# Gating unit of a fused two-block kernel: the bias of the token mixing added by VectorE from a broadcast, in place of one-partition products on TensorE

## What is computed

```
h = gelu(x @ w_in + b_in);  u, v = split(h)
v = layernorm(v) * ln_w + ln_b
vb = v.reshape(4 blocks, 128 tokens j, 8 groups g, 128 columns c)
ws_m = ws with ws[g, i, j] = 0 where chunk(j) > chunk(i)   # chunks of 64 tokens
s[n, i, g, c] = sum_j ws_m[g, i, j] * vb[n, j, g, c] + bs[g, i]
return (u * s) @ w_out
```

## Time and profile of the kernel before

| | |
|---|---|
| Median of 3 runs | 3359.97 us (3358.32 to 3361.44) |
| The profiled execution | 3353.19 us, of which the span is 3351.4 us |
| PE busy (share of the span) | 3183.2 us (95%) |
| DVE busy | 2043.6 us (61%) |
| ACT busy | 1271.1 us (38%) |
| POOL busy | 797.8 us (24%) |
| Granted TensorE clock, mean | 0.968 |

### The profile page before, as it was taken

One profiled execution on the slowest core, in us unless ns is written; L12 is line 12 of the kernel. 1 busy time (PEld: TensorE's weight loads), 2 busy tenths in 40 slices (PEclk: granted clock), 3 DMA queues, 4 the chain that ended last, 5 costly groups with the idle time before them and its releaser, 6 DMA issues.

```text
span 3351.4 us, 42738 instructions
## 1 busy us (share of the span) xinstructions
PE 3183.2 (95%) x16817; PEld 2725.9 (81%) x16817; DVE 2043.6 (61%) x3710; ACT 1271.1 (38%) x2159; POOL 797.8 (24%) x495
## 2 busy tenths in 40 slices
PE   7878999989999999999999999999999997999999
PEld 6456989878888877888878577999999996888777
DVE  5386566564332444333257644888888774887878
ACT  4364444433232333322234433335445452333332
POOL 0000010100000020000000300477676752345553
PEclk9888999999999998999999699999999998999999
DMA  3132221133332321333322012378878888999997
GB/s 119 33 83 65 63 65 58 58 114 88 99 96 95 113 82 57 101 95 96 99 87 81 1 38 89 112 251 296 302 267 314 282 293 297 360 348 356 339 350 276
DMA packets 229210, 537.67 MB, mean 160 GB/s; under 512 B 22337, under 2 KB 88129, under 8 KB 227474
## 3 DMA queue, kind: packets, MB, share of 16 engines
q1 hardware_dynamic: 191570, 398.57, 36.0%
q0 software_dynamic: 37440, 136.36, 11.1%
HBM read 482.40 MB, written 52.46 MB: 160 GB/s over the span
## 4 chain that ended last, share of the span: by engine, by line
PE 70%; DVE 13%; DMA 8%; POOL 3%; ACT 3%; issue 2%; SPq 1%; DVEq 0%; ACTq 0%
PE bank L344 22%; PE bank L347 14%; PE bank L2200 10%; PE bank L2628 5%; DMA gl<-acts 4%; DMA eu<-in_peer_u 3%; POOL etl L2188 3%; PE bank L975 2%; PE bank L2357 2%; DVE vsl L2672 2%; PE bank L985 2%; DVE y_row L2245 2%; PE bank L939 1%; PE bank L1775 1%; PE bank L927 1%
## 5 line engine op out<-in xcount | busy, mean ns | idle before, releaser
L294 DVE TENSOR_TENSOR wl<-raw,wh 128x1024 fp32r<-128x1024 f32 (+3 forms) x239 | 294.1, 1233 | 655.3 <-ACT wh L279 655.2
L279 ACT CAST wh<-raw 128x1024 fp32r<-128x1024 f32 (+3 forms) x239 | 247.3, 1037 | 656.2 <-PE bank L344 359.0
L2188 POOL TENSOR_TENSOR etl<-eu,eth 128x1024 fp32r<-128x1024 f32 x128 | 318.8, 2492 | 435.0 <-ACT eth L2184 434.0
L2200 PE MATMUL bank<-peerhh,eth 128*128 128x384 f32 x1024 | 350.2, 342 | 30.1 <-POOL etl L2188 27.6
L2200 PE MATMUL bank<-peerhh,etl 128*128 128x384 f32 x1024 | 344.0, 336 | 0.0
L2200 PE MATMUL bank<-peerhl,eth 128*128 128x384 f32 x1024 | 344.0, 336 | 0.0
L2628 PE MATMUL bank<-vsh,coefh 128*128 128x512 f32 x768 | 302.1, 393 | 13.9 <-DVE coefl L2683 13.9
L2225 POOL DMA_INDIRECT taken<-in_peer_v,gb x128 | 250.2, 1955 | 262.0 <-DVE y_row L2245 234.7
L2628 PE MATMUL bank<-vsl,coefh 128*128 128x512 f32 x768 | 301.1, 392 | 0.0
L2628 PE MATMUL bank<-vsh,coefl 128*128 128x512 f32 x768 | 301.1, 392 | 0.0
L2184 ACT CAST eth<-eu 128x1024 fp32r<-128x1024 f32 x128 | 135.5, 1060 | 237.0 <-DMA eu<-in_peer_u 237.0
(11 more groups left out here) (544 smaller groups left out, 7457.3 us busy)
## 6 DMA issues: line engine op xcount, KB each, us to landing
eu<-in_peer_u SPq DMA_DIRECT2D x128, 512.0 KB
vb<-in_peer_v SPq DMA_DIRECT2D x128, 512.0 KB
raw<-in_ada_w SPq DMA_DIRECT2D x48, 512.0 KB, 3.8
acts<-eg SPq DMA_DIRECT2D x128, 192.0 KB
coefs<-stage SPq DMA_DIRECT2D x12, 2048.0 KB, 9.6
gd<-coefs SPq DMA_DIRECT2D x16, 1536.0 KB, 14.0
gl<-acts SPq DMA_DIRECT2D x128, 192.0 KB
raw<-in_ffn_w_gate SPq DMA_DIRECT2D x44, 512.0 KB, 3.6
```

The costliest lines, as they stand in the source:

```text
L279: act.copy(parts_of(c)[0], raw_of(c)).then_inc(*up("w rounded", c))
L294: dve.tensor_tensor(lo, raw_of(c), hi.bitcast(F32), ALU.subtract).then_inc(*up("w split", c))
L2188: pool.tensor_tensor(Et[j % 3][1], Eu[j % 2], Et[j % 3][0].bitcast(F32), ALU.subtract).then_inc(*up("u split", j))
L2200: t = pe.matmul(b, tb[un][:, k * 128:(k + 1) * 128], peer_h[hn][:, k, 1:4, :], start=k == 0 and i == 0, stop=k == 7 and i == 2)
```

## The change

The bias row `bsr` on one partition becomes `bsb`, the same 1024 values on all 128 partitions, written by one transfer of 512 KB in place of 4 KB. The 32 one-partition products are gone, and the row of ones with them. DVE gets one step more for each group: it adds the bank and the bias (repeated over the four blocks) into `btmp`, and multiplies from `btmp` in place of the bank. `btmp` has two buffers, and they are those that held v with its input bias. TensorE's bank is free after the addition, where it was free after the multiplication.

```diff
-    bsr, row1 = f("bsr", 120, 1024)[0:1, :], f("row1", 128, 128)[0:1, :]
+    bsb = f("bsb", 120, 1024)
...
-        sp.dma_start(bsr, I["sgu_bs"][0].rearrange("(o g) i -> o (g i)", o=1)).then_inc(*up("sgu in", by=16))
+        sp.dma_start(bsb, I["sgu_bs"][0].rearrange("g i -> (g i)").partition_broadcast(128)).then_inc(
+            *up("sgu in", by=16))
...
-            b, before = banks.take(("sgu s", g), ("sgu gated", g))
+            b, before = banks.take(("sgu s", g), ("dve step", "sgu mixed", g))
...
                 oc = b[:, tt * 128:(tt + 1) * 128]
-                pe.matmul(oc, row1, bsr[:, g * 128:(g + 1) * 128], start=True, stop=False, skip_group_check=True)
-                t = pe.matmul(oc, sgu_v[:, tt, g * 128:(g + 1) * 128], wsT[:, g * 128:(g + 1) * 128], start=False,
-                              stop=True, skip_group_check=True)
+                t = pe.matmul(oc, sgu_v[:, tt, g * 128:(g + 1) * 128], wsT[:, g * 128:(g + 1) * 128], start=True,
+                              stop=True)
...
-                if half == 0:
-                    dve.memset(row1, 1.0)
...
             on_dve.wait_ge(*at("bank full", "sgu mixed", g))
+            if g >= 2:
+                on_dve.wait_ge(*at("sgu gated", g - 2))
+            dve.tensor_tensor(btmp[g % 2].rearrange("p (t i) -> p t i", t=4),
+                              banks["sgu s", g].rearrange("p (t i) -> p t i", t=4),
+                              bsb[:, g * 128:(g + 1) * 128].unsqueeze(1).to_broadcast([128, 4, 128]),
+                              ALU.add).then_inc(*up("dve step", "sgu mixed", g))
+            on_dve.wait_ge(*at("dve step", "sgu mixed", g))
             on_dve.wait_ge(*at("sgu u", g))
-            dve.tensor_tensor(sgu_u[:, g, :], sgu_u[:, g, :], banks["sgu s", g],
+            dve.tensor_tensor(sgu_u[:, g, :], sgu_u[:, g, :], btmp[g % 2],
                               ALU.mult).then_inc(*up("sgu gated", g))
```

## The result

The changed kernel takes 3321.25 us (median of 4 runs, 3318.13 to 3323.63), beside 3360.7 us for the kernel before (4 runs, 3358.32 to 3363.02). The ratio is 0.9882, with a 95% interval of 0.9865 to 0.9899. In a second set of runs, on another occasion, it was 3327.02 us (6 runs) and 0.9895 (0.9874 to 0.9916). The profiled execution took 3321.01 us against 3353.19, so 32.2 us less, while the medians of the first set are 39.5 us apart and those of the second 32.0 (3359.06 before).

A forecast was written before the change was run, and what follows sets the result against it. TensorE alone was taken to bound the mixing stage. Earlier output products 34.6, their faster start 1.7, less a 0.3 wait, gave 36.0 us off the 3359.97 median: 3324.0 us, range 3320 to 3328, or 3318 to 3332 with two rivals.

The forecast's parts named there:

- The bound: Mixing stage: TensorE alone bounds its 42.3 us; the change was forecast to gain 36.0 us in all.
- The pace of what is left: Mixing stage on TensorE: the 32 remaining products take 0.24 us each, 7.7 us in all.
- The rival of 0.41 us without the bias: Mixing products keep 0.41 us each without the bias; stage 13.3 us, time 3329.3 us; chance 0.14.
- The depth changes: Mixing stage on TensorE: each change between depths 1 and 128 costs 0.17 us; all 64 go.
- The clock: TensorE's granted clock, 0.50 from 1250 on before, was forecast to stay at 1.00 in the mixing.
- the slow start of the output products: First nine output products, at the low clock before: 2.1 us in place of 3.8, a gain of 1.7 us.
- The rival of a fall at the same place: TensorE's clock falls again at 1243.4 in the mixing; gain 31.6 us, time 3328.4 us; chance 0.09.
- DVE: Mixing stage: with the added addition a group takes 2.0 us on DVE, against 0.96 us on TensorE.
- The wait for the third piece of weights: Output products: TensorE waits 0.3 us for the output weights' low part on DVE, bounds 0 and 1.5 us.
- The transfer: Bias input: 512 KB in place of 4 KB costs nothing, 4.7 us at most.
- All behind the stage moves as one: After the mixing stage: every later fetch and stage moves earlier by the whole gain, 36.0 us.
- A shift of this kind and size: Later stages (attention, retrieval): where the clock falls shifts, worth some 3 us each way; chance 0.04.

The follow-up runs named there:

- the deep bias products: The kernel before with its bias product made 128 partitions deep in place of 1, nothing else changed; 3336.21 us, ratio 0.9937.

## Why the prediction was right

3324.0 us was forecast and 3321.25 measured, with a range of 3318 to 3332. The mechanism is borne out step by step; that the medians agree to 2.8 us is in part luck, since the second set gave 3327.02, and since the profiled execution, forecast at 3317.2, took 3321.01. Point by point:

- **The bound.** TensorE alone set the stage; taking 64 records away moved the update behind the gating unit by 36.3 us, for a forecast of 36.0.
- **The pace of what is left.** 0.24 us was taken from other lines' products of the same shape; it was 0.221. The 0.234 us came from the length of a group, which counts the modelled end of its last product as well; by the same reading the changed kernel's line gives 7.31 / 32 = 0.228, so about half of the difference is the reading. The stage took 7.1 us, for 7.7 forecast. The rival of 0.41 us without the bias is excluded by this, and by the deep bias products at 0.222.
- **The depth changes.** 0.17 us was read as a difference of two rows, too little by the 0.02 us that the pace was too much; the experiments give 0.19 to 0.20. What TensorE does in that time no run shows.
- **The clock** stayed at 1.00, and the slow start of the output products was gone: the first nine take 2.2 us (1246.57 - 1244.41) where they took 3.8. The rival of a fall at the same place did not come.
- **DVE.** A group was forecast at 2.0 us and is 1.93 (1241.92 - 1239.99, the starts of the second and third additions), since the multiplication starts 0.72 us behind the addition and not 0.8. The wait for the third piece of weights was forecast at 0.3 us and is 0.33; doubling the additions showed that there is no slack behind it.
- **The transfer** of 512 KB cost nothing that shows: the mixing started 1.1 us earlier than before, and the stages ahead of it were as early (1.0 us at the update after the recurrent layer).

Two steps were wrong without harm to the sum. "All behind the stage moves as one" held to the attention only; there the clock stayed low for 10 us more in the profiled execution, and 3 us were lost. A shift of this kind and size was among the rivals, with a chance of 0.04. And the attention was shown beside the mixing as if the two were one case. It is not: 64-deep products that alternate with 128-deep ones kept the clock at 1.00 in the mixing. In the attention the clock fell within a wait of 3.9 us with no product, and then stayed low through products that are 64 deep. The end of that wait in the kernel before:

```profile
1848.91 0.48 PE L1716 MATMUL bank<-ident,p 128*128 128x128 f32 x1 [3.89 <-DVE p L2025]
```

Why it stayed low there, while such products keep it once it is high, is open.

## What to carry to other kernels

A small product on TensorE is not cheap because it is small. A one-partition product that adds a bias costs as much as a full one (0.22 us) and 0.19 us more for the change of shape on either side, and 32 of them among as many full ones halved the clock of this stage; look for pairs of shapes that alternate, and for a granted clock below 1.00 in windows that are fully busy. Group products by shape, put pairs of 64-deep ones on different halves of the partitions next to each other, or move the small operation to an engine that has time, and then count what stands behind it on that engine (here one piece of weights, which came 0.3 us late).

## What the runs showed of the hardware

- TensorE's clock fell to 1.2 GHz while TensorE was busy for 100% of the time and products stood 0.27 us apart, when half of the products were 1 partition deep; also with 32 deep at 0.41 us. It did not with 64 deep, or with 128 deep and 64 columns, at the same loose pace. The depth at which it changes over lies between 32 and 64, where I had not expected it.
- A change between depths costs 0.19 to 0.20 us on TensorE at full clock, whether the other product is 1, 32 or 64 deep; a change of columns costs some 0.17 us.
- Two 64-deep products on the two halves of the partitions run side by side: four records in 0.49 us, where one product's two records take as long.
- Four one-partition products started in four blocks of one bank, with the products that add to them only afterwards, lost the bias: the output was off as without any (a relative 1.431 in both). How was not tried.
